# Where seven RMS norms of a two-block network collect their sums of squares, and which engine reads the banks first

## What is computed

```python
def rms_norm_2(x, g):
    xf = x.astype(jnp.float32)
    y = xf * lax.rsqrt(jnp.mean(xf * xf, axis=-1, keepdims=True) + RMS_EPS)
    return (y * g.astype(jnp.float32)).astype(x.dtype)

    h = h + rms_norm_2(m, mix_post_g[layer])
    f = squared_relu_mlp(rms_norm_2(h, ffn_pre_g[layer]), w_ff1[layer], w_ff2[layer])
    h = h + rms_norm_2(f, ffn_post_g[layer])
```

## Time and profile before

| | us |
|---|---|
| median of 3 runs | 1723.36 (1722.25 to 1725.24) |
| the profiled execution | 1725.55 |
| its span, first to last instruction | 1723.7 |
| TensorE busy | 1703.6 (99%) |
| VectorE busy | 937.7 (54%) |
| ScalarE busy | 606.5 (35%) |
| GpSimd busy | 187.6 (11%) |
| mean granted TensorE clock | 0.997 of full speed |

### The profile page before, as it was taken

One profiled execution on the slowest core, in us unless ns is written; L12 is line 12 of the kernel. 1 busy time (PEld: TensorE's weight loads), 2 busy tenths in 40 slices (PEclk: granted clock), 3 DMA queues, 4 the chain that ended last, 5 costly groups with the idle time before them and its releaser, 6 DMA issues.

```text
span 1723.7 us, 21902 instructions
## 1 busy us (share of the span) xinstructions
PE 1703.6 (99%) x8100; PEld 1364.4 (79%) x8100; DVE 937.7 (54%) x1251; ACT 606.5 (35%) x892; POOL 187.6 (11%) x159
## 2 busy tenths in 40 slices
PE   9999999999999999999999999999999999999998
PEld 7878888888888866587888888888777788888886
DVE  5775546653665399847532343366873653234432
ACT  4564434432444332444321222244553432122221
POOL 0210201100111101111200111100001021001111
PEclk9999999999999999999999999999999999999999
DMA  6211223332333255222333323213201233332321
GB/s 232 74 50 53 95 83 98 93 127 86 97 97 95 81 169 151 75 86 62 110 98 97 96 90 104 92 45 98 73 25 46 77 98 98 98 98 91 94 84 49
DMA packets 48884, 157.92 MB, mean 92 GB/s; under 512 B 7088, under 2 KB 7728, under 8 KB 48816
## 3 DMA queue, kind: packets, MB, share of 16 engines
q1 hardware_dynamic: 48288, 155.52, 29.0%
q10 hardware_dynamic: 528, 1.46, 0.3%
HBM read 146.14 MB, written 2.10 MB: 86 GB/s over the span
## 4 chain that ended last, share of the span: by engine, by line
PE 93%; DVE 4%; ACT 1%; issue 1%; SPq 1%; DMA 0%; DVEq 0%; ACTq 0%
PE bank L1144 27%; PE bank L1145 27%; PE bank L1146 26%; PE bank L1692 2%; PE bank L1295 1%; PE bank L1301 1%; PE bank L1296 1%; PE bank L1188 1%; PE bank L1234 1%; DVE w_lo L1930 1%; SPq L491 1%; PE bank L1859 1%; PE bank L1182 0%; PE bank L1222 0%; DVE pt_lo L2568 0%
## 5 line engine op out<-in xcount | busy, mean ns | idle before, releaser
L1930 DVE TENSOR_TENSOR w_lo<-w_raw,w_hi 128x1024 fp32r<-128x1024 f32 x269 | 346.9, 1291 | 306.0 <-ACT w_hi L687 183.1
L1144 PE MATMUL bank<-a_hi,w_hi 128*128 128x512 f32 x1156 | 457.9, 396 | 0.1
L1145 PE MATMUL bank<-a_lo,w_hi 128*128 128x512 f32 x1156 | 454.2, 393 | 0.0
L1146 PE MATMUL bank<-a_hi,w_lo 128*128 128x512 f32 x1156 | 451.8, 391 | 0.0
L1145 PE MATMUL bank<-g_lo,w_hi 128*128 128x512 f32 x688 | 270.7, 393 | 0.0
L1144 PE MATMUL bank<-g_hi,w_hi 128*128 128x512 f32 x688 | 269.0, 391 | 0.0
L1146 PE MATMUL bank<-g_hi,w_lo 128*128 128x512 f32 x688 | 268.0, 390 | 0.0
L1144 PEld LDWEIGHTS bank<-a_hi,w_hi 128*128 128x128 f32 x1156 | 217.4, 188 | 55.6 <-issue 6.1
L1146 PEld LDWEIGHTS bank<-a_hi,w_lo 128*128 128x128 f32 x1156 | 217.4, 188 | 47.6
L1145 PEld LDWEIGHTS bank<-a_lo,w_hi 128*128 128x128 f32 x1156 | 217.6, 188 | 45.7 <-issue 1.0
L687 ACT ACTIVATE w_hi<-w_raw 128x1024 fp32r<-128x1024 f32 x153 | 159.7, 1050 | 158.2 <-PE bank L1146 144.7
(11 more groups left out here) (289 smaller groups left out, 1805.5 us busy)
## 6 DMA issues: line engine op xcount, KB each, us to landing
w_raw<-in_stream SPq DMA_DIRECT2D x269, 512.0 KB, 3.5
shifted<-u_pad SPq DMA_DIRECT2D x120, 66.5 KB, 2.0
h<-in_xT SPq DMA_DIRECT2D x8, 256.0 KB, 6.0
out<-h SPq DMA_DIRECT2D x8, 256.0 KB, 2.1
cst_b<-in_consts SPq DMA_DIRECT2D x1, 896.0 KB, 9.8
cst_b<-in_consts ACTq DMA_DIRECT2D x1, 896.0 KB, 5.9
shifted<-u_pad ACTq DMA_DIRECT2D x8, 66.5 KB, 2.4
tap_cols<-in_vectors SPq DMA_DIRECT2D x16, 29.8 KB, 1.9
```

The source lines that it names most:

```text
L1144: pe.matmul(out, w0, x0, start=start, stop=False, skip_group_check=loose)
L1145: pe.matmul(out, w0, x1, start=False, stop=False, skip_group_check=loose)
L1146: return pe.matmul(out, w1, x0, start=False, stop=stop, skip_group_check=loose)
L1930: dve.tensor_tensor(w_lo[slot][:, :], w_raw[slot][:, :], f(w_hi[slot][:, :]), ALU.subtract)\
```

## The change

It has three parts. (1) `fold_squares` folds once more, to one tile, and `folded_stat` runs four calls instead of eight. (2) In `ffn` and `pre0` GpSimd adds all seven squares to `ssum`; the new `stat_in_one` runs four calls over it in the middle of the fourth unit, after block 3, and `spread` follows after block 5. (3) In `pw2` and `wo` ScalarE squares the bank itself as soon as the unit is done, with the bias inside the operation (scaled like the rest, in `b_pw2_d`), and VectorE reads the bank after the square; in `after`, `load_sqrt` now stands ahead of the wait of the eighth tile, for `ff2b0` and `ff2b1` also.

```diff
+IN_ONE = ("ffn", "pre0")
...
-        _a += max(_n - 2, 0)
+        _a += _n - 1 if _name in IN_ONE else max(_n - 2, 0)
...
-                for k in range(1, STAT_TILES[name] - 1):
+                for k in range(1, STAT_TILES[name] - (name not in IN_ONE)):
...
-                    act.wait_ge(out_read, TILE0[product] + k + 1)
                     if k == 7:
                         load_sqrt(STAT_NO[stat])
-                    square(stat, k, T(m, k))
+                    if per_tile_units == 1:
+                        act.wait_ge(unit_used, UNIT0[product] + k + 1)
+                        square(stat, k, bank[k % 4][:, :], bias=b_pw2_d[:, k:k + 1] if product == "pw2" else 0.0)
+                    else:
+                        act.wait_ge(out_read, TILE0[product] + k + 1)
+                        square(stat, k, T(m, k))
...
+            def stat_in_one(name):
+
+                pe.wait_ge(sum_added, ADD0[name] + STAT_TILES[name] - 1)
+                pe.wait_ge(r_ready, R_NO[STATS[STAT_NO[name] - 1][0]] + 1)
+                for b in range(NB):
+                    last = pe.matmul(bank[4][:, b:b + 1], T(ssum, b, P), cst[:, ONES:ONES + 1], start=(b == 0),
+                                     stop=(b == NB - 1), skip_group_check=True)
+                last.then_inc(stat_done, 1)
...
-                for k in range(2):
-                    for b in range(NB):
-                        last = pe.matmul(bank[4][:, b:b + 1], T(T(m, k), b, P), cst[:, ONES:ONES + 1],
-                                         start=(k == 0 and b == 0), stop=(k == 1 and b == NB - 1),
-                                         skip_group_check=True)
+                for b in range(NB):
+                    last = pe.matmul(bank[4][:, b:b + 1], T(m, b, P), cst[:, ONES:ONES + 1],
+                                     start=(b == 0), stop=(b == NB - 1), skip_group_check=True)
...
-                        three_tiles(name, a_hi, a_lo, split, split)
+                        three_tiles(name, a_hi, a_lo, split)
...
-                        if split in IN_M and k == 3:
-                            folded_stat(split)
-                        if split in IN_M and k == 5:
+                        if k == 3:
+                            folded_stat(split) if split in IN_M else stat_in_one(split)
+                        if k == 5:
                             spread(split)
...
-            three_tiles("pw1", a_hi, a_lo, "pre0", "pre0")
+            three_tiles("pw1", a_hi, a_lo, "pre0")
...
-                        tile_of_eight(n, n % RING, bank[(2 * k + e) % 4][:, :], a_hi, a_lo)
+                        for i in range(KD):
+                            slot = n % RING
+                            last = three(bank[(2 * k + e) % 4][:, :], T(w_hi[slot], i, P), T(w_lo[slot], i, P),
+                                         T(a_hi, i), T(a_lo, i), i == 0, i == KD - 1)
+                            if 2 * k + e == 3 and i == 3:
+                                stat_in_one("pre0")
+                            if 2 * k + e == 3 and i == 5:
+                                spread("pre0")
+                        last.then_inc(unit_used, 1)
...
-                for w in (4 * SEQ, 2 * SEQ):
+                for w in (4 * SEQ, 2 * SEQ, SEQ):
                     fold = dve.tensor_tensor(m[:, 0:w], m[:, 0:w], m[:, w:2 * w], ALU.add)
-                    if w > 2 * SEQ:
+                    if w > SEQ:
                         link(fold)
...
+            b_pw2 = cols[:, COL0["b_pw2"]:COL0["b_pw2"] + KD]
+            link(dve.tensor_scalar(b_pw2_d, b_pw2, float(D) ** -0.5, None, ALU.mult))
...
-                unit_done(n)
+                dve.wait_ge(sq_ready, SQ0["post0"] + k + 1)
...
-                unit_done(n)
+                dve.wait_ge(sq_ready, SQ0["post1"] + k + 1)
```

More of the change, by code:

```diff
@@ L204, in program @@
         no_sinks = small[:, 0:SWA_H]
+        b_pw2_d = small[:, SWA_H:SWA_H + KD]
         sq_buf = [tmp[4][:, 0:SEQ], tmp[5][:, 0:SEQ]]
@@ L697, in w_hi_loop, with square @@
                 act.activation(w_hi[slot][:, :], w_raw[slot][:, :], ACT.Copy).then_inc(whi_ready, 1)
-            def square(name, k, src, n=D):
+            def square(name, k, src, n=D, bias=0.0):
                 if k == 0:
@@ L709, in square @@
                     dst = sq_buf[(k - 1) % 2]
-                act.activation(dst, src, ACT.Square, scale=float(n) ** -0.5).then_inc(sq_ready, 1)
+                act.activation(dst, src, ACT.Square, scale=float(n) ** -0.5, bias=bias).then_inc(sq_ready, 1)
             def square_in_m(k):
```

## The result

| | before | changed |
|---|---|---|
| median | 1726.62 us (10 runs, 1722.25 to 1731.53) | 1731.53 us (10 runs, 1727.71 to 1738.56) |
| ratio | | 1.0031 (1.0016 to 1.0046), slower, by far less than 2% |
| profiled execution, its span | 1725.55, 1723.7 us | 1736.70, 1734.9 us |

The difference of the medians is 4.9 us, as forecast, but the ratio's interval allows anything from 2.8 to 7.9 us. The time itself, 1731.5, lies above the range (1725.0 to 1730.2). The profiled execution is 11.2 us longer than the one of before, more than the medians are apart. Four of the ten executions lie between 1736.5 and 1738.6, six between 1727.7 and 1732.6.

The account below looks back on a forecast made before the run. TensorE, busy 99% of the span, was taken as the bound. Terms -2.4 + 3.1 + 3.3 - 0.6 - 0.2 = +3.2, plus 1.7 for the clock, gave +4.9 us: median 1728.3 (profiled 1730.5), range 1725.0 to 1730.2.

Parts of the forecast that it names:

- the difference is carried over to that: Base time: median of three runs, 1723.36 us, 2.2 less than the profiled 1725.55; the forecast difference was added to it.
- the sum without the clock: All terms at unchanged clock, folds, `ffn`, `pre0`, squares and square root, together +3.2 us.
- three folds: At mix, ffpre0 and ffpre1: four calls fewer each, VectorE's third fold hidden; 3 x 0.79, -2.4 us.
- `ffn`, clock held: In `upA`: r_pre 3.33 us later, TensorE waits 3.0 us for w_lo at the fifth unit; net +3.1 us.
- `pre0`, clock held: In `pw1`: later r_pre delays the 16 copies and first convolution taps, no slack in the chain; +3.3 us.
- squares, two ends: At post0 and post1: squares ready earlier, but TensorE's 384-column filler limits the gain to 0.3 each; -0.6 us.
- tables of the square root: In both ff2b stages: the one-element square root ahead of the square leaves the path; -0.2 us.
- clock: At the first taps: a 3.8 us wait likely drops the clock, +1.7 us; a drop in `upA` was left open.
- two of the signs that the prediction asked for: Before the first taps: a wait of nearly 4 us for the shifted copies, then a granted clock below 1.
- Slower: Whole kernel: slower than before by more than 0.2% (3.4 us); chance 0.66.
- Rival A: Whole kernel: the clock holds despite the waits; +3.2 us, 1726.6 us; chance 0.28.
- Rival B: In `upA` and at the taps: the clock drops at both; +6.3 us, 1729.7 us; chance 0.17.

Follow-up runs that it names:

- 6 idle: The changed kernel with 14 idle products of 512 columns between upA's fourth and fifth unit; ratio 1.0069 to the kernel before.
- 7 calls: The changed kernel with four narrow calls added behind each of upA, downA and upB; ratio 1.0051 to the kernel before.
- experiment 9: The changed kernel with three idle products of 512 columns between upA's fourth and fifth unit; ratio 0.9996 to the kernel before.
- experiment 4: The kernel before with only the sums and spread of `pre0` moved into the fourth unit of pw1; ratio 1.0016.
- experiment 2: The kernel before with only the squares taken from the banks and the square root's table loaded earlier; ratio 0.9997.
- 1 folds: The kernel before with only the third fold, four sum calls instead of eight; ratio 0.9975.
- 3 ffn: The kernel before with only the sums and spread of `ffn` moved into the fourth unit of upA; ratio 1.0028.
- 5 ahead: The changed kernel with the weights of upA's fifth and sixth unit made ahead of the norm; ratio 0.9998 to the kernel before.
- 8 sums: The kernel before with GpSimd adding all seven squares of `ffn` and `pre0`, the sum calls left behind the first unit; ratio 0.9997.
- 10 no idle: The kernel before with squares from the banks and no idle product of 384 columns between the sums at post0 and post1; ratio 0.9993.
- experiment 11: The changed kernel with weights made ahead in upA and pw1, and pw1's small reduction ahead of the norm; ratio 0.9973 to the kernel before.
- experiment 12: The kernel before with third fold, unmoved merged sums, bank squares without the idle product, and pw1's weights and reduction ahead; ratio 0.9953, median 1719.56 us.

## Why the prediction was wrong, point by point

**The time.** The step that failed is the one ahead of the sum: "the difference is carried over to that", the median of three runs, 1723.36. Ten runs of the same kernel have the median 1726.62, and 35, 23 and 35 more in the three batches 1725.93, 1725.05 and 1727.76. The forecast of +4.9 us on 1726.62 would have been 1731.5. And the range held only the bounds of the terms. The spread of the executions was to be seen in none of my views, since three runs within 3 us of each other don't show that 23 of 93 lie above 1729 us. Why the three were among the faster ones stays open.

**The difference.** That it came out at 4.9 us to the decimal is luck. Its interval is 2.8 to 7.9 us. And two errors stand against each other: the sum without the clock was too high by 0.4 us (with copies of nearly equal length, experiments 6 and 7), and the sum had one clock drop, where the traces mostly have two.

**The sum.** Its terms and what the traces show:

| term | forecast | measured |
|---|---|---|
| three folds | -2.4 | -2.7 (3 x 0.89) |
| `ffn`, clock held | +3.1 | +3.2 (experiment 9) |
| `pre0`, clock held | +3.3 | +3.2 at the first copy; at the taps +2.2 (experiment 4) to +3.1 (experiments 6 and 7) |
| squares, two ends | -0.6 | -0.6 (experiment 2: 0.32 and 0.26) |
| tables of the square root | -0.2 | -0.2 (experiment 2: 0.09 and 0.07) |
| clock | +1.7, at the taps | +1.0 in `upA`, +1.3 to +1.7 at the taps, where it drops |

- *Folds*: right in kind, mis-sized by 0.1 each: sixteen narrow instructions in a row take 1.68 and eight take 0.79, so the eight that go are worth 0.89. At pre0's and ffn's sums the same 0.9 was won. In all these rows an instruction costs 98 to 111 ns. The Trainium skill puts a floor of about 25 ns under narrow products (TensorE: Matmul & The Clock Gate, "Wait — 56ns, not 53.3ns?"), by which eight would be 0.2 us, an estimate; these calls stay well above that floor.
- *`ffn`*: right step by step. w_lo was to end at 240.73 and does at 241.24, less the 0.6 of shift that was there before, 240.64. TensorE waited 3.25 us for it, where 3.0 was forecast. In the change the next w_lo is covered by the slowed unit; in experiment 9 it is not.
- *`pre0`*: the chain was right to the first copy (+3.2). At the taps the term was mis-sized wherever the copies were shorter: I took one execution's 11.39 us for the price, but it is the longest of fourteen traces, and sixteen copies take 10.39 to 11.39 us from one execution to the next. That is also why the profile after has no wait of nearly 4 us and no drop at the taps, two of the signs that the prediction asked for; with copies of 11.30 us both are there.
- *Squares and tables*: right, and right in the reason, the idle product.
- *Clock*: right that a wait of about 3 us can drop it, wrong in which: the drop in `upA`, left open and out of the sum, came in all three traces with that wait, the one at the taps in six of seven. The price of 1.7 us was read from the drop near 122, but there it cost only 0.9: in the four traces without it the shift falls by 0.86 at that place. At the taps it cost 1.3 to 1.7.

**The chances.** "Slower", 0.66, came true by the ratio itself, 1.0031; its interval reaches a little below the 0.2% that the prediction drew. Rival A (the clock holds) is the kernel without drops: +2.8 us by the measured terms with copies of nearly equal length, +1.9 with those of experiment 4. Rival B (it drops at both places), given 0.17, is what most traces show: the two drops add 2.3 to 2.7. The 233 ns pace adds, in some executions, up to 6.9.

## The chance in the executions

The clock record of each trace, drops of 3.4 us each (6.8 where doubled), and the stretches at 233.3 ns:

| profiled run | near 122 (wait 2.59 in all) | near 160 | fifth unit (wait) | taps (wait) | 233 ns pace |
|---|---|---|---|---|---|
| before | yes | no | no (0) | no (1.54) | 787 to 797, 1363 to 1373 |
| changed | yes | yes | yes (3.25) | no (2.86) | 246 to 609 |
| 1 folds | no | no | no (0) | no (1.08) | |
| 2 squares | yes | no | no (0) | no (1.15) | 331 to 599 |
| 3 ffn | yes | yes | yes (3.24) | no (0.76) | |
| 4 pre0 | yes | no | no (0) | yes (2.80) | |
| 5 ahead | yes | no | no (0) | yes (2.99) | |
| 6 idle | yes | no | no (0) | yes (3.72) | |
| 7 calls | no | no | yes (3.25) | yes (3.70) | 174 to 232, 795 to 807 |
| 8 sums | no | no | no (0) | no (0.97) | 781 to 792 |
| 9 three idle | yes | yes | no (0.68) | yes (2.78) | 357 to 606 |
| 10 no idle | yes | yes | no (0) | no (1.10) | 784 to 797 |
| 11 all ahead | yes | yes | no (0) | yes (2.72) | |
| 12 best | no | no | no (0) | no (0) | 1357 to 1368 |

(Stretches of 40 products or more; the start of every trace, 8 to 27 us, runs at 233 ns too.) The table leaves out a drop near 720, behind the convolution, where narrow calls and idle products stand. It lasts 6.8 us in nine traces, before and the changed kernel among them, 3.4 in four (experiments 6, 8, 9 and 10) and is missing in experiment 2. Against before the shift between 700 and 740 us falls by 1.1 to 1.6 us where the drop is the short one and by 2.2 where there is none, so this place alone makes single executions differ by 2 us. Two more drops stand alone: experiment 9 at 1311, experiment 12 at 701 behind a wait of 2.24 us, while the wait of 2.28 us at the same place in experiment 11 had none.

Near 122 the wait is that of the earlier trace rows in all fourteen, and the clock dropped in ten. Experiment 1 kept it:

```profile
121.00:123.00 2.00, 1.21 (x9) 1.17 (x10) 1.97 (x6) 2.00 (x10) 0.00 (x0) 1.00 0.00 0
123.00:126.00 3.00, 2.53 (x12) 1.73 (x10) 2.96 (x9) 2.44 (x4) 0.00 (x0) 1.00 0.54 171
```

The waits of 2.7 to 3.7 us at the fifth unit and at the taps dropped it nine times out of ten, and the changed kernel's at the taps is the tenth; the waits under 1.6 us at these two places never did. The drop near 160 has no wait of its own: TensorE works there without a pause in all of them. It goes with the drop before it, though: it is there in the five traces in which the clock fell 0.6 to 1.3 us after TensorE had resumed near 122, and in none of the five in which it fell by 0.2 us after that or earlier. So the drops of one execution are not independent of each other.

The 233 ns pace was found in long stretches of dense products in four traces (some 250 to 1560 products). Each of these ended where narrow calls stand: at 232, 599, 606 and 609 us, the sums of `ffn` and `pre0`. The six short ones in the table end at narrow calls too, the sums of `ffpre0` and `ffpre1`, and the start of each trace at those of the first norm. What sets it in stays open: in the changed kernel it began as the clock came back, in experiments 2 and 9 in the middle of the products with nothing to see. Nor is it shown that the change makes it likelier: 4 of 10 executions of the change are in the upper group, but 7 of 35, 3 of 23 and 13 of 35 of the kernel before lie above 1729 us in the three batches.

## What to carry to other kernels

Before sums of a norm are moved later, read what the other engines have queued behind its factor: here two weight pieces behind r_pre cost 3.2 us of TensorE, and making them earlier took nearly all of it back. Merge work (here seven squares on an idle engine) where the result stands now, before moving it as well: it gave the whole 0.9 us each time, while the move gave only loss, 0.3 us at `ffn` even with the weights made ahead. And when an effect is 0.3% of the time, compare the starts of the same products in two traces place by place, and take the base from as many runs as the forecast will be held against.

## What was not expected of the hardware

- Two paces of dense products at the same granted clock, 228.9 and 233.3 ns, lasting for up to 363 us and worth up to 6.9 us. Every stretch that was found ended at narrow calls.
- Behind a wait of 2.59 us, the same in each execution, the clock is down for 3.4 us in ten of fourteen and stays up in four.
- One of sixteen equal copies on the SP queue took 1.59 us instead of 0.59; the sixteen vary by 1.0 us between executions.
- An idle product of 512 columns in full float32 costs 0.86 us, 3.7 times one of the kernel's own products.
